# The RWKV scan: its triangular inverses taken from TensorE's five levels to a substitution on GpSimd

## The chip, the cores and the metric

The kernel runs on one core of a Trainium2 chip. The metric is the device time of one execution in microseconds (us), the median of the runs.

## The reference, cut to what matters

The program is two transformer blocks in a row. The part changed is the RWKV-7 layer: 16 heads of 64 features, 768 tokens (256 of context, then 512), scanned in both directions.

```python
def step(S, inp):
    w_t, k_t, v_t, kk_t, a_t = inp[:5]
    s_kk = jnp.einsum('nbhvk,nbhk->nbhv', S, kk_t)
    S = S * w_t[..., None, :] - s_kk[..., :, None] * (kk_t * a_t)[..., None, :] + v_t[..., :, None] * k_t[..., None, :]
    y_t = jnp.einsum('nbhvk,nbhk->nbhv', S, inp[5]) if emit else None
    return S, y_t
s_final, ys = lax.scan(step, state0, seqs)
```

The kernel does this by chunks of 64 tokens (CH). Within a chunk the dependence of each token on those before it is a unit triangular 64x64 matrix, which has to be inverted once for every head, chunk and direction: 16 x 12 x 2 of them.

## The kernel before, in words

The program is a list of stages. All engines meet between two stages (stage_done, L2995); the SP queue, which only issues DMAs, runs ahead as far as its own waits allow.

**RwkvTerms** (L2291) goes over 8 pairs of heads, m = 0 to 7 (KD). For each it makes five factors of 128x768 for either direction (decays, keys, values) and stores them to DRAM as "terms". DVE does `terms(m)` and then `factors(m+1)` (L2560); TensorE does `lora`, `norm` and `bonus` of m+1 (L2459); ACT does the exponentials and sigmoids; GpSimd does `directed` and `weighted` (L2396 to L2411); SP stores (L2364 to L2377). At the end GpSimd waits for the stores (L2428).

**RwkvScan** (L2577) makes 24 passes, three to a pair of heads. A pass n has four chunks (BATCH) in both directions d. The two heads of a pair sit on partitions 0 to 63 and 64 to 127, so each product is two 64x64 matmuls (`heads`, L2680), and `each` (L2685) does it for the four chunks: 8 matmuls. Every fp32 matmul is two instructions in the trace. In `make` (L2698) TensorE computes the products of the terms, then transposes by the identity (L2717 to L2720), and then inverts: LEVELS has five levels (2, 4, 8, 16, 32), and at each the inverse T and its transpose TT are doubled in block size by a product z (L2727), which DVE masks (L2826), and the products for T (L2737) and TT (L2738), which DVE adds (L2832, L2834). The last level needs TT alone. Then come w (L2741) and the two corrections (L2744, L2745), and DVE makes nh_h, qa and a (L2839 to L2842).

The recurrence itself is `step` (L2747): four steps per pass, each 16 matmuls, whose new state DVE scales (L2859) before the next step can run. The four steps of pass n-1 are spread between the levels of pass n, so that one fills the waits of the other; `alone` does the last four. The order is written out by hand in `make` of each engine; the instructions of one engine run in that order.

SP loads the terms of a pass in five parts of 256 KB, waiting for each (L2665 to L2669), into one of three buffers. It waits before a pass for `taken` (L2663), which DVE raises at the end of a pass (L2845), so it can be up to three passes ahead. At the start of the stage GpSimd clears the output (L2672), and DVE raises the first `taken` only behind that (L2791, L2792).

Of the kernel before, what the change touches and what calls it, by code (L numbers as in the profile page):

```python
# [47 lines left out]
CH = 64  # L48
NC = T // CH
# [152 lines left out]
def scan_constants():  # L202
# [5 lines left out]
    off = lambda s: (r // (2 * s) == c // (2 * s)) & (r // s != c // s)  # L208
    starts = np.broadcast_to(np.arange(T) % CH != 0, (P, T)).astype(np.float32)
    masks = [lo, up, r >= c, r <= c, -1.0 * (lo & off(1)), -1.0 * (up & off(1)), r == c] + [-1.0 * off(s) for s in (2, 4, 8, 16, 32)]  # L210
    return np.ascontiguousarray(np.concatenate([starts] + [two(x) for x in masks], 1))
# [2079 lines left out]
class RwkvTerms(Stage):  # L2291
# [8 lines left out]
    def __init__(self, chip):  # L2300
# [4 lines left out]
        self.starts, at = chip.view(at, T), at + T  # L2305
# [17 lines left out]
        assert at + 4 * P <= A_W  # L2323
        self.decays = chip.view(DECAYS, KD, 2, NC)
# [3 lines left out]
        self.bonus_stored = [chip.sem(f"terms_bonus_stored{u}") for u in range(2)]  # L2328
        (self.starts_in, self.scaled, self.sliced, self.lora, self.activated, self.raw_done, self.squared,
# [6 lines left out]
    STORED = 4 * 16  # L2336

# [16 lines left out]
    def sync(self, sp):  # L2354
        d = self.chip.dram
        sp.wait_ge(self.chip.stage_done, 4 * self.index)
        sp.dma_start(self.starts, d["scan_const"][:, 0:T]).then_inc(self.starts_in, 16)
# [6 lines left out]
        def store(m, u, i, more):  # L2364
# [11 lines left out]
            for b, chunks in enumerate((0, 2, 1)):  # L2376
                sp.dma_start(to[b, :, 1], flat[1][:, chunks]).then_inc(self.stored[u], 16)  # L2377

# [8 lines left out]
    def gpsimd(self, pool):  # L2387
# [40 lines left out]
        for u in range(2):  # L2428
            pool.wait_ge(self.stored[u], self.STORED * (KD // 2) + self.STORED)
            pool.wait_ge(self.bonus_stored[u], 16 * (KD // 2))  # L2430

    def tensor(self, pe):
# [30 lines left out]

        def step(m, u, i, more):
            first(m + 1, 1 - u, i)

        self.w.landed(pe, 0, 0)
        self.each(pe, first, step, nothing)
# [49 lines left out]
    def vector(self, dve):  # L2518
# [40 lines left out]

        def step(m, u, i, more):  # L2560
            terms(m, u, i)
            factors(m + 1, 1 - u, i + u)

        self.each(dve, factors, step, terms)


Y_RWKV = A_HL
LEVELS = (2, 4, 8, 16, 32)
SCAN_MASKS = ["lo", "up", "lo_diag", "up_diag", "lo1", "up1", "ident64"] + [f"level{s}" for s in LEVELS]
# [7 lines left out]
class RwkvScan(Stage):  # L2577

    def __init__(self, chip):
# [5 lines left out]
        self.t, self.tt, self.z, self.qa, self.a, self.lbt = (single(i) for i in range(6))  # L2587
        self.v = [single(i) for i in range(6, 6 + BATCHES)]
        at += (12 + 2 * BATCHES) * BATCH * CH
        double = lambda i: [chip.view(at + (2 * i + d) * BATCH * 2 * CH, BATCH, 2, CH) for d in range(2)]  # L2590
        self.p_lg, self.mb_b, self.mg_g, self.w, self.nh_h = (double(i) for i in range(5))
        at += 10 * BATCH * 2 * CH
# [464 lines left out]
```

## Time and profile before

| | |
|---|---|
| median of 3 runs | 6093.58 us (6093.32 to 6096.73) |
| the profiled execution | 6084.52 us, span 6082.9 us |
| mean granted TensorE clock | 0.935 |
| busy share of the span | PE 88%, DVE 41%, ACT 20%, POOL 7% |
| chain that ended last | PE 70%, DVE 8%, issue 7% |
| RwkvTerms | from 3237.9 us (its first DMA) to 3495.9 us |
| RwkvScan | from 3495.9 us to 4285.5 us |

PE is TensorE, DVE VectorE, ACT ScalarE, POOL GpSimd and SP the queue that issues DMAs. The span is that of the profiled execution, from its first to its last instruction.

### The profile page before, as it was taken

The numbers are of one execution on the slowest core, as the hardware profiler recorded it, in microseconds if no ns is written. First come the engines' busy times: TensorE is split into PE (matmuls) and PEld (weight loads), VectorE is DVE, ScalarE is ACT, GpSimd is POOL, SyncE is SP. The second block draws the span as 40 slices with busy tenths as digits, with TensorE's granted clock in tenths as the row PEclk, the third lists the DMA queues.
The fourth block names the chain that finished last, engine by engine and source line by source line (L and its number), as shares of the span: only waits on it lengthen the run. The fifth ranks groups of instructions, "written<-read, shape, count | busy, mean of one in ns | idle before, by whom it ended". The sixth has DMA issues, their size and how long they took to land.

```text
span 6082.9 us, 89797 instructions
## 1 busy us (share of the span) xinstructions
PE 5368.0 (88%) x36014; PEld 3112.2 (51%) x36014; DVE 2479.6 (41%) x4422; ACT 1212.2 (20%) x1969; POOL 429.9 (7%) x397
## 2 busy tenths in 40 slices
PE   7977878899999899987995389999688999999999
PEld 3556535544444345544552189999343444444443
DVE  2357644511231216733105867777514445411110
ACT  2113213300121111101004400011112333311120
POOL 0014200000000001100003400000100000000000
PEclk9989988899999999998996699999798999999999
DMA  3311330021222113420223521111110000022121
GB/s 137 101 63 69 107 104 13 35 97 55 73 76 76 48 63 131 157 90 31 82 91 141 198 60 44 47 47 30 56 45 32 19 20 17 13 69 76 61 73 69
DMA packets 92899, 428.13 MB, mean 70 GB/s; under 512 B 9952, under 2 KB 10080, under 8 KB 75104
## 3 DMA queue, kind: packets, MB, share of 16 engines
q1 hardware_dynamic: 71072, 338.34, 15.8%
q0 software_dynamic: 21568, 85.99, 4.1%
q8 instruction: 204, 3.34, 0.2%
q14 instruction: 55, 0.45, 0.0%
HBM read 364.53 MB, written 59.77 MB: 70 GB/s over the span
## 4 chain that ended last, share of the span: by engine, by line
PE 70%; DVE 8%; issue 7%; PEld 5%; DVEq 4%; DMA 3%; ACT 2%; PEldq 0%; POOL 0%; POOLq 0%; ACTq 0%; SPq 0%
PE psum L371 42%; PE psum L2682 12%; PE psum L2253 6%; PEld psum L371 4%; PE psum L1979 2%; PE psum L1978 2%; PE psum L633 1%; DMA sbuf<-w_side 1%; PE psum L2001 1%; DVEq L2530 1%; DVEq L2540 1%; PE psum L1014 1%; PE psum L1259 1%; DVE sbuf L648 1%; DVE sbuf L2956 1%
## 5 line engine op out<-in xcount | busy, mean ns | idle before, releaser
L371 PE MATMUL psum<-sbuf 128*128 128x512 f32 (+4 forms) x8640 | 3214.3, 532 | 210.3 <-DVEq L1470 61.8
L371 PEld LDWEIGHTS psum<-sbuf 128*128 128x128 f32 (+1 forms) x8640 | 1573.9, 192 | 1816.3 <-issue 1584.1
L2682 PE MATMUL psum<-sbuf 64*64 64x64 f32 (+1 forms) x21504 | 757.4, 228 | 58.7 <-SPq L2669 47.3
L2682 PEld LDWEIGHTS psum<-sbuf 64*64 64x64 f32 x21504 | 740.5, 134 | 76.2 <-issue 62.5
L2253 PE MATMUL psum<-sbuf 128*128 128x512 f32 (+1 forms) x1088 | 358.1, 490 | 30.8 <-DVE sbuf L2233 29.0
L1476 DVE SCALAR_TENSOR_TENSOR sbuf<-psum,sbuf 128x512 f32 x64 | 42.3, 682 | 660.1 <-PE psum L371 660.1
L2253 PEld LDWEIGHTS psum<-sbuf 128*128 128x128 f32 x1088 | 207.3, 191 | 181.6 <-issue 163.9
L583 DVE CUSTOM_DVE_ANT_0 sbuf<-sbuf 128x1024 f32<-128x1024 f32 x160 | 212.2, 1327 | 36.4 <-DMA sbuf<-w_side 15.8
L2772 ACT ACTIVATE sbuf<-psum 128x256 f32<-128x256 f32 x192 | 76.2, 438 | 728.7 <-PE psum L2682 727.5
L2437 PE MATMUL psum<-sbuf 64*128 64x512 f32 (+2 forms) x192 | 92.1, 739 | 145.5 <-ACT sbuf L2491 68.4
L616 ACT ACTIVATE sbuf<-sbuf 128x512 f32<-128x512 f32 (+1 forms) x114 | 53.0, 551 | 667.7 <-DVEq L2999 649.1
L664 DVE TENSOR_SCALAR sbuf<-sbuf 128x512 f32<-128x512 f32 (+1 forms) x68 | 36.2, 533 | 331.3 <-ACT sbuf L1522 189.0
L1696 POOL TENSOR_TENSOR sbuf<-sbuf 128x768 f32<-128x768 f32 (+1 forms) x32 | 45.2, 1415 | 1543.9 <-DVEq L1758 1330.7
L2095 DVE TENSOR_REDUCE sbuf<-psum 128x1 f32<-128x768 f32 x64 | 61.3, 958 | 211.4 <-PE psum L1979 211.4
L2437 PEld LDWEIGHTS psum<-sbuf 64*128 64x128 f32 (+1 forms) x192 | 40.8, 276 | 196.5 <-ACT sbuf L2491 73.1
L1746 ACT ACT_TABLE_LOAD x32 | 41.1, 1283 | 494.0 <-PEq L1731 494.0
L573 POOL DMA_DIRECT2D sbuf<-w_side x128 | 68.5, 535 | 864.6 <-DVE sbuf L583 860.8
L633 PE MATMUL psum<-sbuf 128*128 128x512 f32 (+1 forms) x228 | 92.8, 565 | 34.0 <-ACT sbuf L616 34.0
L1768 DVE SCALAR_TENSOR_TENSOR sbuf<-psum,sbuf 128x512 f32<-128x512 f32 (+1 forms) x48 | 30.3, 659 | 225.2 <-PEq L1731 220.4
L1978 PE MATMUL psum<-sbuf 128*128 128x512 f32 (+1 forms) x256 | 117.3, 541 | 3.5 <-DVE sbuf L2086 3.5
L1979 PE MATMUL psum<-sbuf 64*128 64x512 f32 (+1 forms) x256 | 119.8, 549 | 0.0
L1649 DVE TENSOR_TENSOR sbuf<-sbuf 128x512 f32 x40 | 27.7, 693 | 224.4 <-ACT sbuf L1639 224.4
(274 smaller groups left out, 4876.9 us busy)
## 6 DMA issues: line engine op xcount, KB each, us to landing
sbuf<-w_side POOLq DMA_DIRECT2D x128, 512.0 KB, 3.9
sbuf<-w_sgu_uz SPq DMA_DIRECT2D x32, 1088.0 KB, 5.0
sbuf<-terms SPq DMA_DIRECT2D x120, 256.0 KB, 2.7
sbuf<-w_up SPq DMA_DIRECT2D x22, 1024.0 KB, 4.9
sbuf<-w_merge SPq DMA_DIRECT2D x8, 2560.0 KB, 8.9
sbuf<-w_sgu_v SPq DMA_DIRECT2D x8, 2048.0 KB, 7.9
sbuf<-w_sgu_out SPq DMA_DIRECT2D x16, 1024.0 KB, 4.8
terms<-sbuf SPq DMA_DIRECT2D x8, 1920.0 KB, 11.4
```

The lines of the kernel that those rows point to most:

```text
L371: last = nc.tensor.matmul(out, w, x, start=(n == 0), stop=(n == len(pairs) - 1))
L573: pool.dma_start(self.slot[b], src).then_inc(self.landed[b], 16)
L583: last = v.tensor_tensor_reduce(junk, self.slot[b], self.rows[:, c], 1.0, 0.0, ALU.mult, ALU.add, self.sums[:, b, n:n + 1])
L633: last = self.nc.tensor.matmul(self.chip.bank(n, t), self.chip.const("ones"), squares[:, i], start=(i == 0), stop=(i == k - 1))
L648: v.reciprocal(inv, rms)
L1978: t.matmul(s[:, a:a + w], self.qn[u][:, q], self.kn[u][:, a:a + w], start=True, stop=False)
L1979: last = t.matmul(s[:, a:a + w], rot[:, q], self.kr[u][:, a:a + w], start=False, stop=True)
L2095: v.tensor_reduce(self.mx[:, n:n + 1], self.s_bank(n), AX.X, ALU.max)
L2253: last = self.nc.tensor.matmul(self.wide(b)[:, at:at + width], w[:, k], xs[:, k, at:at + width], start=(k == 0), stop=(k == KD - 1))
L2437: last = t.matmul(out[:, at:at + width], w, x[:, at:at + width], start=True, stop=True)
L2682: last = t.matmul(out[hs], lhs[hs], rhs[hs], start=start, stop=stop)
L2772: copy = lambda to, of: a.activation(to, of, ACT.Copy)
```

## The change

In RwkvTerms TensorE also makes, for each pair of heads, the two diagonal 32x32 blocks of every 64x64 triangle (12 chunks, 2 directions, 2 heads, 2 blocks: 96 matmuls with 64 rows, 32 columns and 32 elements moved). DVE masks and negates them in one operation of 128x768, and SP stores them to DRAM in four DMAs, whose contiguous runs are 32 elements (128 B).

In RwkvScan the 96 blocks of a pair are loaded so that each lies in one partition (32 x 32 elements). `substitute` inverts all of them in place by substitution: 30 steps of a product and a sum, with a drain behind either, and a transposed copy at the end. GpSimd does it for pairs 1 to 7, one pair ahead, and DVE for pair 0 at the start of the stage. SP stores both results to DRAM (384 KB each), waits, and loads them back into the layout of the matmuls with 12 DMAs of 32 partitions x 12 chunks x 128 B. `terms` in SP's new order is the load of one pass as before. TensorE keeps the level of 32 alone, as two products of 32x32 blocks, whose results ACT copies; the products of the terms are put in another order, and ACT takes over some copies. All four steps of the recurrence still stand between the parts of the next pass, and DVE raises the first `taken` before GpSimd's clearing. The masks, the smaller buffers and the new semaphores are left out of the diff:

```diff
@@ RwkvTerms.sync, at the end of store(m, u, i, more)
+            sp.wait_ge(self.blocks_out, m + 2)
+            for q in range(4):
+                sp.dma_start(blocks[q], self.blocks[u][BLK * q:BLK * q + BLK]).then_inc(self.blocks_stored[u], 16)
@@ RwkvTerms.gpsimd, at the end
+            pool.wait_ge(self.blocks_stored[u], self.BLOCKS_STORED * (KD // 2) + self.BLOCKS_STORED)
@@ RwkvTerms.tensor
+                    if (q, d) == (1, 0) and not (isinstance(m, int) and m == 0):
+                        pe.wait_ge(self.blocks_out, m)
...
+        def blocks(m, u):
+            pe.wait_ge(self.done, m + 2)
+            pe.sem_inc(self.pe_waited, 1)
+            for d, (row, col) in enumerate(((0, 2), (2, 0))):
+                o = self.out[u][d]
+                for c in range(NC):
+                    for r in range(2):
+                        for h in range(2):
+                            hs, rows, cols = slice(CH * h, CH * h + CH), CH * h + BLK * r, BLK * (NC * d + c)
+                            b = slice(BLK * r, BLK * r + BLK)
+                            last = t.matmul(self.wide(3)[rows:rows + BLK, cols:cols + BLK], o[hs, c, row, b], o[hs, c, col, b], start=True, stop=True)
+            last.then_inc(self.block_sums, 1)
+
         def step(m, u, i, more):
             first(m + 1, 1 - u, i)
+            pe.wait_ge(self.activated, 4 * m + 7)
+            pe.sem_inc(self.pe_waited, 1)
+            blocks(m, u)
@@ RwkvTerms.vector
+        def blocks(m, u, i):
+            dve.wait_ge(self.blocks_stored[u], self.BLOCKS_STORED * i + self.BLOCKS_STORED)
+            dve.wait_ge(self.block_sums, m + 1)
+            v.tensor_tensor(self.blocks[u], self.wide(3).rearrange("p (k c) -> p k c", c=BLK), across(self.strict, NBLK), ALU.mult
+                            ).then_inc(self.blocks_out, 1)
+
         def step(m, u, i, more):
             terms(m, u, i)
             factors(m + 1, 1 - u, i + u)
+            blocks(m, u, i)
@@ RwkvScan.sync
+        sp.dma_start(self.x[0], d["blocks"][0]).then_inc(self.blocks_in[0], 16)
...
+        def inverse(m):
+            u = m % 2
+            if m == 0:
+                sp.wait_ge(self.first_inverse, 1)
+            else:
+                sp.wait_ge(self.inverse_ready, m)
+            sp.dma_start(d["inverse"][m, 0], self.x[u]).then_inc(self.inverse_stored, 16)
+            sp.dma_start(d["inverse"][m, 1], self.xt[u]).then_inc(self.inverse_stored, 16)
+            sp.wait_ge(self.inverse_stored, 32 * m + 32)
+            back = [d["inverse"][m, i].rearrange("(q k) (i c) -> q i k c", q=4, c=BLK) for i in range(2)]
+            for way in range(2):
+                chunks = slice(NC * way, NC * way + NC)
+                for q in range(4):
+                    to = slice(BLK * q, BLK * q + BLK)
+                    if q % 2 == way:
+                        sp.dma_start(self.t[u][to, chunks], back[way][q, :, chunks]).then_inc(self.inverse_in[u], 16)
+                    sp.dma_start(self.tt[u][to, chunks, self.cols(q % 2)], back[1 - way][q, :, chunks]).then_inc(self.inverse_in[u], 16)
+
+        for m in range(KD):
+            terms(m, 0)
+            terms(m, 1)
+            inverse(m)
+            if m + 1 < KD:
+                sp.dma_start(self.x[(m + 1) % 2], d["blocks"][m + 1]).then_inc(self.blocks_in[(m + 1) % 2], 16)
+            terms(m, 2)
@@ RwkvScan, new method
+    def substitute(self, eng, engine, m, products):
+        x = self.x[m % 2].rearrange("p (i c) -> p i c", c=BLK)
+        xt = self.xt[m % 2].rearrange("p (i c) -> p i c", c=BLK)
+        eng.wait_ge(self.blocks_in[m % 2], 16 * (m // 2) + 16)
+        engine.memset(self.x[m % 2][:, 0:BLK * BLK:BLK + 1], 1.0)
+        for j in range(1, BLK - 1):
+            n = BLK - 1 - j
+            left = x[:, j + 1:BLK, j:j + 1].broadcast_to([4 * NBLK, n, j])
+            right = x[:, j:j + 1, 0:j].broadcast_to([4 * NBLK, n, j])
+            product = products[0:4 * NBLK, 0:n * j].rearrange("p (i c) -> p i c", c=j)
+            engine.tensor_tensor(product, left, right, ALU.mult)
+            eng.drain()
+            engine.tensor_tensor(x[:, j + 1:BLK, 0:j], x[:, j + 1:BLK, 0:j], product, ALU.add)
+            eng.drain()
+        engine.tensor_copy(xt, x.rearrange("p i c -> p c i"))
@@ RwkvScan.gpsimd
+        for m in range(1, KD):
+            self.substitute(pool, self.nc.gpsimd, m, products)
+            pool.drain().then_inc(self.inverse_ready, 1)
@@ RwkvScan.tensor, make (the removed lines are those of the listing)
+                if past:
+                    wait(self.w_out[d], n)
+                each(at(self.half(d, 1, 0)), term(0), term(3))
+                each(at(self.half(d, 1, 1)), term(3), term(1)).then_inc(self.sums[d], 1)
...
                 wait(self.made[d], n + 1)
+                each(flat(self.slots(d, 0, 2)), term(2), pq).then_inc(self.sums[d], 1)
+                each(at(self.half(d, 2, 0)), term(0), id64)
+                each(at(self.half(d, 2, 1)), term(4), id64).then_inc(self.sums[d], 1)
             if past:
                 step(*past, 0)
...
+                wait(self.evacuated[d], 2 * n + 2)
+                each(at(self.half(d, 0, 0)), term(2), id64)
+                each(at(self.half(d, 0, 1)), term(3), id64).then_inc(self.token_sums[d], 1)
+            if past:
+                step(*past, 1)
+            if pos == 0:
+                wait(self.inverse_in[m % 2], self.INVERSE_IN * (m // 2) + self.INVERSE_IN)
...
+            for s in range(BATCH):
+                for h in range(2):
+                    for d in range(2):
+                        rows = self.rows(h, d)
+                        last = t.matmul(self.narrow(d, 1)[self.rows(h, 1 - d), s], self.lbt[d][rows, s], inverse[0][d][rows, s], start=True, stop=True)
...
+            if past:
+                step(*past, 2)
             for d in range(2):
+                wait(self.z_out[d], n + 1)
+                wait(self.copied[d], n + 1)
+            for s in range(BATCH):
+                for h in range(2):
+                    for d in range(2):
+                        rows = self.rows(h, 1 - d)
+                        last = t.matmul(self.narrow(d, 2)[self.rows(h, d), s], self.z[d][rows, s], inverse[1][d][rows, s, self.cols(1 - d)], start=True, stop=True)
...
+            if past:
+                step(*past, 3)
             for d in range(2):
+                wait(self.tt_out[d], n + 1)
+                each(flat(self.slots(d, 1, 2)), at(inverse[1][d]), flat(self.p_lg[d])).then_inc(self.w_sums[d], 1)
```

On ACT each pass now copies term 0 and term 4 (128x256, twice for each direction), the two token transposes, z (128x128), the two 32-row halves of the new block of TT, and w (128x512). DVE keeps the masks of the four products of a pass, one of them (lbt) now 128x128, then the four steps, then nh_h, qa and a.

## Rows read from the trace of the kernel before

**Rows 1.** Busy time by stretch: span, then us and (instructions) of PE, PEld, DVE, ACT, POOL; PEclk, DMA share, GB/s.
```profile
3495.00:3515.50 20.50, 0.00 (x0) 0.00 (x0) 0.00 (x0) 0.00 (x0) 5.22 (x1) 0.50 0.30 85
...
3600.00:3700.00 100.00, 98.85 (x2830) 96.78 (x2832) 74.55 (x197) 9.54 (x24) 0.00 (x0) 1.00 0.16 43
```

**Rows 2.** Scan, groups by line and shape: count, busy us, mean ns, idle before.
```profile
L2682 PE MATMUL psum<-sbuf 64*64 64x64 f32 x17664 | 546.9, 218 | 10.3 <-DVEq L2843 1.2 <-issue 1.1 <-DVE sbuf L2859 0.8
L2682 PE MATMUL psum<-sbuf 64*64 64x128 f32 x3840 | 222.7, 271 | 48.4 <-SPq L2669 47.3
L2826 DVE TENSOR_TENSOR sbuf<-psum,sbuf 128x256 f32<-128x256 f32 x240 | 102.0, 425 | 14.1 <-PE psum L2682 2.8
L2772 ACT ACTIVATE sbuf<-psum 128x256 f32<-128x256 f32 x144 | 47.4, 384 | 301.4 <-PE psum L2682 300.2
L2839 DVE TENSOR_TENSOR sbuf<-sbuf,psum 128x512 f32<-128x512 f32 x48 | 33.1, 689 | 65.7 <-PE psum L2682 65.7
```

**Rows 3.** Timeline of the last steps, done alone (start us, us, engine, line).
```profile
4279.06 1.15 PE L2682 MATMUL psum<-sbuf 64*64 64x64 f32 x32 [1.19 <-DVEq L2843]
4279.86 0.48 DVE L2859 TENSOR_SCALAR sbuf<-psum,sbuf 128x64 f32<-128x64 f32 x2 [1.19 <-PE psum L2682]
...
4280.48 1.15 PE L2682 MATMUL psum<-sbuf 64*64 64x64 f32 x32 [0.27 <-DVE sbuf L2859]
```

**Rows 4.** Lines L869 and L1321, GpSimd: ns min/median/max, first and last start.
```profile
L869 POOL TENSOR_TENSOR sbuf<-sbuf x40: 1031/1042/1045, 390.3 to 480.4; 128x512 f32<-128x512 f32 x40
...
L1321 POOL TENSOR_TENSOR sbuf<-sbuf x12: 1261/1274/1732, 881.3 to 1160.2; 128x512 f32<-128x512 f32 x12
```

**Rows 5.** Timeline of GpSimd in the stage behind the scan.
```profile
4301.48 1.81 POOL L2971 TENSOR_TENSOR sbuf<-sbuf 128x768 f32 x1 [799.80 <-DVE sbuf L2960]
4303.45 1.81 POOL L2973 TENSOR_TENSOR sbuf<-sbuf 128x768 f32 x1 [0.16 <-issue]
```

**Rows 6.** Timeline of an early stage: GpSimd and DVE side by side.
```profile
520.09 1.28 POOL L970 TENSOR_TENSOR sbuf<-sbuf 128x512 f32<-128x512 f32 x1 [0.92 <-ACT sbuf L985]
...
520.15 1.13 DVE L1076 SCALAR_TENSOR_TENSOR sbuf<-psum,sbuf 128x128 f32<-128x128 f32 x4 [0.43 <-PE psum L1014]
```

**Rows 7.** Scan, groups by shape: a DVE operation with both inputs in SBUF.
```profile
L2810 DVE TENSOR_TENSOR sbuf<-sbuf 128x256 f32<-128x256 f32 x48 | 20.5, 426 | 5.3 <-issue 0.9
```

**Rows 8.** DMA issues: count, KB each, median us from issue to landing.
```profile
sbuf<-terms SPq DMA_DIRECT2D x120, 256.0 KB, 2.7
...
bonus<-sbuf SPq DMA_DIRECT2D x8, 384.0 KB, 2.3
```

**Rows 9.** DMA queue q1, 3240 to 3495 us: packets, MB, share of 16 engines.
```profile
q1 hardware_dynamic: 12212, 48.34, 49.5%
```

**Rows 10.** The same queue, 3495 to 4290 us.
```profile
q1 hardware_dynamic: 17740, 32.70, 14.5%
```

**Rows 11.** Busy time of one stretch of RwkvTerms, columns as in Rows 1.
```profile
3330.00:3360.00 30.00, 10.65 (x24) 4.67 (x24) 28.89 (x18) 18.31 (x23) 15.10 (x7) 0.61 0.52 197
```

**Rows 12.** Timeline of RwkvTerms, one turn of m.
```profile
3338.35 2.93 PE L2437 MATMUL psum<-sbuf 128*128 128x512 f32 x4 [8.94 <-ACT sbuf L2491]
...
3348.96 6.17 PE L2437 MATMUL psum<-sbuf 128*128 128x512 f32 x16 [7.68 <-POOL sbuf L2408]
...
3352.17 0.96 DVE L2541 TENSOR_TENSOR sbuf<-sbuf 128x768 f32<-128x768 f32 x1
...
3353.32 2.52 DVE L2549 TENSOR_TENSOR sbuf<-sbuf 128x768 f32<-128x768 f32 x1 [0.19 <-issue]
```

**Rows 13.** The chain that ended last, end of RwkvTerms and start of RwkvScan.
```profile
3483.71 0.33 SPq L2371
...
3486.40 9.25 DMA terms<-sbuf
...
3496.45 5.29 POOLq L2673
```

More of the change, by code:

```diff
@@ L2323, in __init__ @@
         assert at + 4 * P <= A_W
+        assert self.w.words + 2 * NBLK * BLK <= WSLOT
+        at = A_W + self.w.slot(0) * WSLOT + self.w.words
+        self.blocks = [chip.view(at + u * NBLK * BLK, NBLK, BLK) for u in range(2)]
         self.decays = chip.view(DECAYS, KD, 2, NC)
@@ L2562, in step, with last @@
             factors(m + 1, 1 - u, i + u)
-        self.each(dve, factors, step, terms)
+            blocks(m, u, i)
+        def last(m, u, i):
+            terms(m, u, i)
+            blocks(m, u, i)
+        dve.sem_inc(self.blocks_out, 1)
+        for u in range(2):
+            dve.sem_inc(self.blocks_stored[u], self.BLOCKS_STORED)
+        self.each(dve, factors, step, last)
 Y_RWKV = A_HL
-LEVELS = (2, 4, 8, 16, 32)
-SCAN_MASKS = ["lo", "up", "lo_diag", "up_diag", "lo1", "up1", "ident64"] + [f"level{s}" for s in LEVELS]
+SCAN_MASKS = ["lo_diag", "up_diag", "lo", "up", "ident64"]
 HEAD = [slice(CH * h, CH * h + CH) for h in range(2)]
@@ new lines, in sync, with terms @@
+        sp.dma_start(self.chip.view(self.masks_at, len(SCAN_MASKS) * CH), d["scan_const"][:, T + BLK:]).then_inc(self.masks_in, 16)
+        def terms(m, b):
+            sp.wait_ge(self.taken, 3 * m + b + 1)
+            src = d["terms"][3 * m + b].rearrange("p d w -> p (d w)")
+            for part in range(PARTS):
+                w = slice(part * LOAD, part * LOAD + LOAD)
+                sp.dma_start(self.terms[:, b, w], src[:, w]).then_inc(self.landed, 16)
+                sp.wait_ge(self.landed, (48 * m + 16 * b) * PARTS + 16 * part + 16)
+            sp.sem_inc(self.ready, 1)
@@ new lines, in make @@
+            inverse = [[self.of_pass(x, m, pos, d) for d in range(2)] for x in (self.t, self.tt)]
+            for d in range(2):
+                wait(self.evacuated[d], 2 * n + 1)
+            for s in range(BATCH):
[3 more added lines that the diff above has]
+                        last = t.matmul(self.narrow(d, 1)[self.rows(h, 1 - d), s], self.lbt[d][rows, s], inverse[0][d][rows, s], start=True, stop=True)
+                        if (s, h) == (BATCH - 1, 1):
+                            last.then_inc(self.z_sums[d], 1)
@@ L2766, in alone @@
                 step(*past, s)
-        self.passes(pe, make, alone, written_out=True)
+        self.passes(make, alone)
     def scalar(self, act):
@@ new lines, in make @@
+                dve.wait_ge(self.sums[d], 3 * n + 1)
+                v.tensor_tensor(self.p_lg[d][:, :, 1], self.half(d, 1, 0), self.mask(after[d]), mult)
+                v.tensor_tensor(self.mg_g[d][:, :, 0], self.half(d, 1, 1), self.mask(before[d] + "_diag"), mult)
+            for d in range(2):
+                dve.wait_ge(self.sums[d], 3 * n + 2)
+                lbt = self.slots(d, 0, 2)
+                v.tensor_scalar(self.lbt[d], lbt[:, :, 0, self.cols(1 - d)], -1.0, None, mult).then_inc(self.evacuated[d], 1)
+                v.tensor_tensor(self.mb_b[d][:, :, 0], lbt[:, :, 1], self.mask(before[d] + "_diag"), mult).then_inc(self.evacuated[d], 1)
@@ L2872, in alone @@
                 step(*past, s)
-        self.passes(dve, make, alone, written_out=True)
+        self.passes(make, alone)
 class RwkvOutput(Stage):
```

222 lines of the change are left out of this document (99 added, 123 removed).

## The prediction

> **What bounds the kernel now.** I read the busy times by stretch first, to find the stage that the change is about, then the groups by shape within it. In the scan's steady part TensorE is busy 98.85 us of 100, at the full granted clock, with DVE at 75 and ACT at 10 [rows 1]. The groups by shape say what fills it: 17,664 instructions on 64 columns, 31.0 ns of TensorE each (546.9 us over the count), and 3,840 on 128 columns, 58.0 ns each [rows 2]. A pass is a 24th of that, 736 and 160 instructions: 22.8 + 9.3 = 32.1 us, and TensorE's busy stretch, 770 us, divided by 24 gives the same. So the scan is bound by TensorE's count of instructions, and no wait in it matters but the first 20 us, where everything waits for the first terms [rows 1]. The timeline of the last steps shows what hides behind that: done alone, a step comes every 1.42 us with 1.15 us of TensorE in it [rows 3].
>
> The chain that ended last shows the seam before the scan: DVE's last terms are done at 3483.7, the last store lands at 3495.6, then GpSimd clears the output for 5.3 us, and SP's first load waits for that [rows 13]. In RwkvTerms DVE is busy 28.89 us of 30, TensorE 10.65 at a clock of 0.61 [rows 11]: DVE bounds that stage.
>
> **TensorE in the scan.** Counted from the code, in instructions (two to a matmul), the 64-column ones of a pass fall from 736 to 320 (64 for the products of two terms, 64 for transposes of terms 0 and 4, 64 for the two token transposes, 128 for the four steps), the 128-column ones from 160 to 128 (the product with two terms, w, two corrections). New are 64 on 32x32 blocks. The trace has none such; 31 ns is one end, a third of it, 10 ns, the other, and I take 20, as four of them lie on separate quarters of the array where 64x64 ones lie on two. The pass: 320 x 31.0 + 128 x 58.0 + 64 x 20 = 9.9 + 7.4 + 1.3 = 18.6 us.
>
> The waits inside a pass: z, ACT's copy, the second product, ACT's two copies for each direction, w, copy, corrections. A step of 1.15 us stands in each of the first gaps. A result reaches its reader about 0.23 us after the last matmul (DVE starts 0.80 us after a step's first, whose first half takes 0.57) [rows 3], and ACT's copies are under 0.38 us each [rows 2]. The gap behind z needs 0.23 + 2 x 0.3, covered; that behind the second product needs 0.23 + 4 x 0.25, some 0.1 over. With 0.3 for each of a few step boundaries I add 1.1 us: 19.7 a pass, 59 us for a pair of heads. DVE needs 8 masks of about 0.42, eight state scalings of 0.24, two additions and six operations behind the corrections: some 10 us of these 19.7 [rows 2, 3]. ACT needs 7. Neither bounds.
>
> Within the pass the 32x32 products change the shape of the tile four times. No row here shows such a change between products of these two shapes. If each emptied the array, at the 0.23 us above, a pass would be 20.6 us.
>
> The Trainium skill (TensorEngine Tiling (Array Packing), Key Properties) says that changing the tiling mode, not just the tile, drains TensorE. By it a pair would take 62 us on TensorE; since another loop turns out longer, the sum below would rise by about 3 us only, in the passes at both ends.
>
> **GpSimd's substitution.** 30 steps, with products and sums of j(31-j) elements each: 4,960 elements in either, 60 operations with a drain behind each. On GpSimd a plain two-input operation takes 1.274 us for 512 elements [rows 4] and 1.81 for 768 [rows 5]: 2.09 ns an element and 0.20 fixed. With one operand broadcast, as the product's is, 512 take 1.042 [rows 4]: 1.64 ns. Behind a drain the next starts 0.16 us later [rows 5]. So 4,960 x 1.64 + 4,960 x 2.09 = 18.5, 60 x 0.36 = 21.6, and 2 for the transposed copy: 42 us. The unknown is what short rows cost: 930 rows of 1 to 30 elements in all. L869 has eight rows; were its fixed 0.20 all due to them, a row costs 25 ns, and the total is 42 - 12 + 23 = 53. Below, 38 if the drain's gap overlaps. I take 42, by the rows. DVE beside it slows GpSimd only where both read two operands from SBUF: beside L1076, with one in PSUM, GpSimd's 1.28 us equals 1.274 [rows 6, 4], and DVE's operations in the new passes have one input in PSUM.
>
> **The DMAs.** The loads of a pass take 5 x 2.7 = 13.5 us of SP [rows 8]. New for each pair: two stores of 384 KB, 2.3 us [rows 8], 3 with their issues; 12 loads that are 4,608 runs of 128 B; a load of 384 KB. No row has runs of 128 B. The terms stage's queue gives 49.5% x 255 x 16 / 12,212 = 165 ns for a packet of 3.96 KB [rows 9], the scan's 14.5% x 795 x 16 / 17,740 = 104 ns for 1.84 KB [rows 10]: 29 ns a KB and 51 ns fixed, so 55 ns for 128 B, and 4,608 x 55 / 16 = 16 us. The ends are 4 us (12 issues of 0.33) and 30 (104 ns each). I take 16.
>
> **The loops.** (a) TensorE: 59. (b) GpSimd: substitution 42, then stores 3, the loads back 16, and behind them in the same queue the next pair's blocks 2.7: 64. SP can ask for those blocks only then. (c) SP: when pass 3m-2 ends it loads terms (m,1) for 13.5, stores 3, loads back 16; then the pass that waits has 10 left and one more of 19.7: 62. So 64 us a pair, with 96 before.
>
> **The start.** DVE clears TT (two of 1,536, at most 3.5 us) and substitutes pair 0: 9,920 x 1.04 ns and 60 x (0.16 + 0.10), from 0.426 us for 256 [rows 7] and 0.96 for 768 [rows 12], 27 us with the copy. SP, which no longer waits for GpSimd's clearing, has loaded two passes in the same 27 us. Then 3 + 16 + 1: the first inverse is in at about 3547; before, the first pass ended there. The end: 3547 + 7 x 64, then 10 + 2 x 19.7 for the last pair and 6.5 alone, is 4051, against 4285.5: -234.5 us.
>
> **RwkvTerms.** TensorE makes the blocks behind `bonus` of the next pair. That starts at 3348.96 and takes 2.9 us, as `norm` does for the same shapes [rows 12]. 192 instructions of 31 ns are 6 us (ends: 2, and 12 at the half clock that this stage mostly has [rows 11]). DVE, done at 3353.1 [rows 12], waits until 3358.1 and adds 1.0 us for its mask. In exchange GpSimd's two products run in that wait, and DVE's next two operations no longer take 2.5 us beside them but 0.96 [rows 12]: -3.1. Net 5.0 + 1.0 - 3.1 = 2.9 a turn, 20 us for seven (0 to 62). What was queued behind on DVE, `terms(m+1)`, is what waits. The tail: blocks 6, mask 1.2, then 3,072 runs behind the terms' stores, 10.6 us: the stage ends some 10 us later than by the chain of before [rows 13]. Together +30 (5 to 80).
>
> **Sum.** -234.5 + 30 = -204. The profiled execution's 6084.5 becomes 5880; it lies 9 us under the median shown, and against that median I forecast 5890.
>
> **Rivals.** *Small runs cost more* (chance 0.15): at 104 ns they take 30 us, the loop 78, the first inverse comes 14 later, the tail 9: 4163 in place of 4051, so about 6011. For it: nothing shows such packets; against: the line through the two rows. *The pass is latency bound* (0.1): the former cover of five levels is gone, every handover now stands once; at 24 us a pass the pair takes 72, end 4116, time 5955. For it: [rows 3]; against: the steps still stand between. *Rows cost up to 25 ns* (0.12): substitution 53, loop 75, 5967. *Slower* (0.08): short rows are dear on GpSimd, each in a pattern of its own. Break-even is where 7 more loops use up 204 us: 29 us a pair, substitution 71, 31 ns a row; at 50 ns a row it takes 88, the loop 110, and the time is 6212. TensorE then idles at `inverse_in`. Against it: L869's eight rows leave at most 25.
>
> The Trainium skill (GPSIMD Engine Reference, Performance pitfalls) gives about 102 cycles for each small read command, which does not overlap the last. If each row were such a command, the estimate from that page is 85 ns a row and a loop near 143 us. No run here shows such rows.
>
> **Numbers.** Forecast as worked out, or better, 0.55. Better: with quick loads the first inverse is in at 3535 and the loop is 59 (a): 4004, terms +5, -276, 5818. The range 5810 to 6020 takes in this and the first three rivals. About 0.2% is what a measurement of this kernel can tell from no change: faster 0.90, same 0.02, slower 0.08.
>
> **What would show it.** Right: TensorE's instructions in the scan 12,288; a pair of heads every 59 to 66 us; GpSimd's substitutions about 42 us each and busy two thirds of the scan; TensorE's busy share of it falling to some 85%; waits of DVE for TensorE of some 5 us a turn in RwkvTerms. Wrong: single operations on GpSimd well over 0.7 us with their gaps, TensorE waiting long for a DMA onto the inverse once in three passes, or gaps behind every product of a pass.

## The result, and the profile after

The changed kernel takes 5812.38 us, the median of 4 runs (5804.21 to 5822.77), against 6093.45 for the kernel before (4 runs): a ratio of 0.9539, with a 95% interval of 0.9524 to 0.9554. The profiled execution took 5804.21, with a span of 5801.8; before, the span was 6082.9. The forecast was 5890, with a range of 5810 to 6020, so the time lies 2 us inside the range's lower end, and two of the four runs lie below it: 281 us were gained where 204 had been worked out.

All of it is inside the two stages concerned. The next stage starts on TensorE at 4004.5 instead of 4285.5, 281 us earlier, and nothing behind it moved. The scan starts with its first DMA at 3500.0, 4.1 us later than before. So up to there the changed kernel is 4.1 us behind, and the scan gave 285.1. The terms stage itself takes 264.4 us instead of 258.0, from its first DMA at 3235.6 to 3500.0; it started 2.3 us earlier than before, which the change has no part in.

The busy times by stretch, in the profile after (columns as in [rows 1]):

```profile
3600.00:3700.00 100.00, 92.93 (x2609) 90.61 (x2605) 42.44 (x126) 27.01 (x81) 60.25 (x117) 0.95 0.38 100
3600.00:3900.00 300.00, 279.49 (x7871) 272.79 (x7869) 128.13 (x378) 83.26 (x249) 164.14 (x321) 0.95 0.40 103
```

TensorE was busy 98.85 us of these 100 before [rows 1]; it is now busy 92.93, at a granted clock of 0.95 instead of 1.00. DVE fell from 74.55 to 42.44. So something waits now that did not. The groups of the scan, by shape (to be set against [rows 2]; TensorE's own 64-column and 128-column forms are left together here, as the page has them, for their spans overlap):

```profile
L2805 PE MATMUL psum<-sbuf 64*64 64x64 f32 (+1 forms) x10752 | 422.9, 238 | 39.7 <-SPq L2743 28.1
...
L2865 PE MATMUL psum<-sbuf 32*32 32x32 f32 x768 | 12.5, 205 | 1.6 <-issue 0.9 <-ACT sbuf L2904 0.8
L2853 PE MATMUL psum<-sbuf 32*32 32x32 f32 x768 | 11.9, 203 | 30.9 <-DMA sbuf<-inverse 30.9
```

10,752 + 768 + 768 is 12,288 instructions, the number that was counted from the code; before there were 21,504. They take 422.9 + 12.5 + 11.9 = 447 us, 18.6 for a pass at the mean. And TensorE waits 30.9 us for a DMA onto the inverse: 8 times, once for each pair of heads. The timeline of TensorE around one such wait (start, length, instruction, count, and in brackets the wait ahead of it):

```profile
3662.07 0.65 PE L2853 MATMUL psum<-sbuf 32*32 32x32 f32 x32 [3.76 <-DMA sbuf<-inverse]
3662.66 1.97 PE L2805 MATMUL psum<-sbuf 64*64 64x64 f32 x32
3664.56 0.65 PE L2865 MATMUL psum<-sbuf 32*32 32x32 f32 x32
3665.14 17.09 PE L2805 MATMUL psum<-sbuf 64*64 64x64 f32 x416
3682.16 0.45 PE L2853 MATMUL psum<-sbuf 32*32 32x32 f32 x32
3682.54 1.15 PE L2805 MATMUL psum<-sbuf 64*64 64x64 f32 x32
3683.62 0.45 PE L2865 MATMUL psum<-sbuf 32*32 32x32 f32 x32
3684.00 15.76 PE L2805 MATMUL psum<-sbuf 64*64 64x64 f32 x416
3699.70 0.45 PE L2853 MATMUL psum<-sbuf 32*32 32x32 f32 x32
```

From 3682.16 to 3699.70 lies a pass that nothing disturbs: 17.54 us, with no gap in it. The pass that follows the wait takes 20.09 (3662.07 to 3682.16). The busy times by stretch say why; the column that counts is the third from the end, the granted clock:

```profile
3662.10:3668.00 5.90, 5.90 (x140) 5.66 (x142) 1.63 (x6) 1.52 (x6) 2.60 (x9) 0.50 0.49 144
3668.00:3674.00 6.00, 6.00 (x129) 5.87 (x127) 3.04 (x7) 1.19 (x2) 4.70 (x10) 1.00 0.33 90
```

After 3.76 us without work TensorE is granted 0.50, the lower of its two levels (1.2 GHz), for about 6 us, and then 1.00 again. So this wait costs 3.76 us itself and 2.55 by the clock. Three passes of 17.54 are 52.6; a pair of heads takes 58.2 (the first product with an inverse starts at 3543.96 for pair 0 and at 3951.30 for pair 7, a seventh of the difference).

What TensorE waits for is at the end of SP's work for the pair. The timeline of SP, the same columns (issues without a wait of their own between them are drawn together):

```profile
3541.95 44.11 SPq L2741 DMA_DIRECT2D sbuf<-terms  x15
3588.72 0.34 SPq L2751 DMA_DIRECT2D inverse<-sbuf  x1
3589.10 0.43 SPq L2752 DMA_DIRECT2D inverse<-sbuf  x1
3593.16 0.32 SPq L2760 DMA_DIRECT2D sbuf<-inverse  x1
...
3599.95 0.47 SPq L2761 DMA_DIRECT2D sbuf<-inverse  x1
3600.46 1.18 SPq L2768 DMA_DIRECT2D sbuf<-blocks  x1
3601.68 6.82 SPq L2741 DMA_DIRECT2D sbuf<-terms  x3
```

and what SP waited for in the scan (total, times, longest):

```profile
SPq L2741 <- DMA sbuf<-terms: 251.3, 96, 4.2
SPq L2743 <- DMA sbuf<-terms: 61.3, 24, 3.2
...
SPq L2760 <- DMA inverse<-sbuf: 29.5, 8, 5.1
SPq L2741 <- DVEq L2972: 3.0, 4, 1.6
```

SP never rests. It issues a part of the terms, waits until it has landed, issues the next: 15 parts in the 46.8 us from 3541.95 to 3588.72, 3.1 each. The stores are waited for until 3593.16 (4.4), the loads back and the blocks' load are issued until 3601.6 (8.5), and the next part follows at once. That is 59.7 us for this pair, where the mean pair takes 58.2. For `taken`, which says that a buffer is free, it waits 3.0 us in the whole scan. GpSimd in the meantime:

```profile
3545.61 0.15 POOL L2777 MEMSET sbuf<- 96x32 f32 x1 [39.82 <-DMA sbuf<-blocks]
3545.69 0.24 POOL L2783 TENSOR_TENSOR sbuf<-sbuf 96x30 f32<-96x30 f32 x1
3546.07 0.26 POOL L2785 TENSOR_TENSOR sbuf<-sbuf 96x30 f32<-96x30 f32 x1
```

The substitution runs from 3545.6 to 3586.2, 40.6 us (40.7 in most pairs), and GpSimd then waits 18.6 for its next blocks. SP came to the store at 3588.7, 2.5 us after the inverse was ready, and in the whole scan it never waits for GpSimd there. So in this profile it is not GpSimd's loop that sets the pair but SP's own list of waited transfers, which the prediction had added up only in part. That is the theory which the experiments below test; its rivals are GpSimd's loop, as forecast, and the short runs of the loads back.

In the terms stage the profile after shows:

```profile
3348.22 2.93 PE L2452 MATMUL psum<-sbuf 128*128 128x512 f32 x4 [7.69 <-POOL sbuf L2422]
3351.07 2.79 PE L2493 MATMUL psum<-sbuf 64*32 64x32 f32 x192
...
3351.42 0.96 DVE L2576 TENSOR_TENSOR sbuf<-sbuf 128x768 f32<-128x768 f32 x1
3354.00 0.96 DVE L2598 TENSOR_TENSOR sbuf<-psum,sbuf 128x768 f32<-128x768 f32 x1 [1.62 <-PE psum L2493]
```

The 192 instructions for the blocks take 2.79 us, 14.5 ns each at a granted clock of 0.50, and DVE waits 1.62 for them in this turn. In the turn where the clock was 0.90 they take 1.99, 10.4 ns each.

### The profile page after: what moved, and what is told of

The parts are those of the page before. It is cut to its first block, busy times and chain, and to the rows that moved or that the text cites. A ratio compares the mean times of both kernels' runs of the same rounds, so it can differ in the third digit from the quotient of the medians.

```text
span 5801.8 us, 74255 instructions
## 1 busy us (share of the span) xinstructions
PE 5067.3 (87%) x28334; PEld 2816.2 (49%) x28334; DVE 2134.7 (37%) x3582; ACT 1263.7 (22%) x2161; POOL 650.0 (11%) x831
## 4 chain that ended last, share of the span: by engine, by line
PE 65%; issue 9%; DVE 7%; DMA 7%; PEld 5%; ACT 2%; DVEq 2%; POOL 1%; SPq 1%; POOLq 1%; PEldq 0%; ACTq 0%
PE psum L373 44%; PE psum L2255 6%; PEld psum L373 5%; DMA sbuf<-terms 3%; PE psum L2805 3%; PE psum L1981 2%; PE psum L1980 2%; PE psum L635 1%; DMA sbuf<-w_side 1%; PE psum L2003 1%; PE psum L1016 1%; DVE sbuf L650 1%; PE psum L1261 1%; DVE sbuf L3083 1%; SPq L2761 1%
## 5 line engine op out<-in xcount | busy, mean ns | idle before, releaser
L2805 PE MATMUL psum<-sbuf 64*64 64x64 f32 (+1 forms) x10752 | 422.9, 238 | 39.7 <-SPq L2743 28.1
L2805 PEld LDWEIGHTS psum<-sbuf 64*64 64x64 f32 x10752 | 411.9, 138 | 46.3 <-issue 33.0
L1478 DVE SCALAR_TENSOR_TENSOR sbuf<-psum,sbuf 128x512 f32 x64 | 42.3, 682 | 660.9 <-PE psum L373 660.9
L2904 ACT ACTIVATE sbuf<-psum 128x256 f32<-128x256 f32 (+3 forms) x384 | 128.5, 368 | 395.1 <-PE psum L2805 315.3
L2785 POOL TENSOR_TENSOR sbuf<-sbuf 96x30 f32<-96x30 f32 (+14 forms) x210 | 109.1, 520 | 30.4 <-issue 0.9
```

The source lines that it names most:

```text
L2785: engine.tensor_tensor(x[:, j + 1:BLK, 0:j], x[:, j + 1:BLK, 0:j], product, ALU.add)
L2805: last = t.matmul(out[hs], lhs[hs], rhs[hs], start=start, stop=stop)
L2904: copy = lambda to, of: a.activation(to, of, ACT.Copy)
```

## The experiments

The stages ahead of the scan differ in length between executions (the first product with an inverse starts between 3540 and 3560 in the profiles), and the times of one kernel spread over 13 to 35 us. So beside the time of each kernel the table has, from its profile, the scan's own length from that product to the next stage's first matmul.

| kernel | time, us | ratio to before, 95% | scan, us | PE waits for the inverse, us | POOL waits for blocks, us |
|---|---|---|---|---|---|
| changed kernel | 5812.38 | 0.9539 (0.9524 to 0.9554) | 460.6 | 30.9 | 144.7 |
| one wait a pass (e2) | 5800.23 | 0.9534 (0.9513 to 0.9554) | 450.2 | 19.0 | 133.1 |
| half the substitution (e3) | 5821.09 | 0.9551 (0.9534 to 0.9569) | 459.4 | 25.8 | 256.2 |
| both of these (e4) | 5800.29 | 0.9507 (0.9486 to 0.9527) | 439.4 | 7.3 | 231.9 |
| blocks a pair sooner (e5) | 5812.39 | 0.9527 (0.9510 to 0.9544) | 465.5 | 35.7 | 84.9 |
| one wait, blocks sooner (e6) | 5794.02 | 0.9504 (0.9491 to 0.9518) | 438.3 | 8.9 | 56.7 |
| long runs (e7, one run) | 5797.72 | | 457.1 | 27.9 | 137.1 |

Of the waits for the inverse the first, ahead of pair 0 (8.9 us in the changed kernel), lies ahead of the scan's own length. Each ratio is to the runs of the kernel before that were made beside it; the ratios, and not the medians, are to be compared between rows.

**The terms stage alone (e1).** RwkvTerms of the changed kernel with the scan of the kernel before, which does not read the blocks.

```diff
 class RwkvTerms: as in the changed kernel
 class RwkvScan: as in the kernel before (LEVELS and the masks too)
```

> The kernel of before with the new RwkvTerms alone: the blocks are made and stored, the scan inverts as before and never reads them. My step (TensorE's 192 instructions delay DVE by 5 us a turn, net 2.9, tail 10) gives +30 us on before, about 6123. The rival, read from the trace of the changed kernel (192 instructions take 2.8 us, DVE waits 1.6 and gets its time back because GpSimd's two products no longer run beside it; the stage ends 4 us later), gives +4 us, about 6097.

Measured: 6102.23 us, the median of 12 runs, against 6092.02 (17 runs); ratio 1.0014, 1.0002 to 1.0026, which is 8.5 us, from 1 to 16. The +30 of the prediction is refuted. The turns explain it, read from the profile of the changed kernel: SP's issues of `bonus` stand 29.4 or 29.6 us apart before (3306.13, 3335.70, 3365.09) and 29.5 to 29.7 after (3334.95, 3364.50, 3394.17), but for one turn of 30.9 (from 3304.05); the last turn is 30.5 in both. In e1's own profile that one turn is 32.0 and the others are as before. DVE's groups in the terms stage show the trade, before and after:

```profile
L2550 DVE TENSOR_TENSOR sbuf<-sbuf 128x768 f32<-128x768 f32 x16 | 28.1, 1754 | 0.0
L2549 DVE TENSOR_TENSOR sbuf<-sbuf 128x768 f32<-128x768 f32 x16 | 26.5, 1655 | 2.8 <-issue 2.4 <-ACT sbuf L2507 0.4
```

```profile
L2584 DVE TENSOR_TENSOR sbuf<-sbuf 128x768 f32<-128x768 f32 x16 | 21.9, 1366 | 0.4 <-ACT sbuf L2542 0.4
L2585 DVE TENSOR_TENSOR sbuf<-sbuf 128x768 f32<-128x768 f32 x16 | 20.0, 1251 | 0.0
...
L2598 DVE TENSOR_TENSOR sbuf<-psum,sbuf 128x768 f32<-128x768 f32 x8 | 7.7, 958 | 16.7 <-PE psum L2493 16.7
```

These are the same two operations, whose span beside GpSimd's products is long. The waits (16.7) and the new mask (7.7) add 24.4 us in eight turns; the two groups lose 54.6 - 41.9 = 12.7, and DVE's idle time ahead of them another 2.4. Of the 9.3 us that remain, 7 are the wait and the mask behind the last pair's terms, in the tail, and some 2 lie in the seven turns, most of them in the long one. In that turn TensorE stops for 1.56 us in the midst of the blocks (2.66 in e1), and in the tail for 2.71, and waits for nothing that the profile shows; see below.

**Twice the blocks' matmuls (e8).** If DVE's time beside GpSimd pays part of each wait back, doubling the wait's cause must cost less than its own length.

```diff
@@ tensor, blocks(m, u), on top of e1
-            for d, (row, col) in enumerate(((0, 2), (2, 0))):
+            for d, (row, col) in 2 * list(enumerate(((0, 2), (2, 0)))):
```

> The kernel of before with the new RwkvTerms alone, whose block matmuls are issued twice (384 instructions a turn). Theory of the trade (what DVE waits for TensorE it gets back from GpSimd, whose two products run meanwhile, and by now only 1 us of that is left): 2.8 us more of TensorE, 1.8 us more a turn. Without a trade: 2.8 us more a turn. The tail grows by 2.8 in both.

Measured, in one run: 6122.27. Four turns are undisturbed. In them the 384 instructions take 4.17 to 4.68 us, 4.46 at the mean, where 192 take 2.00 to 2.79 in e1, 2.45 at the mean: 2.0 us more, and not the 2.8 of the expectation. The turns take 29.9 to 30.4 us, 30.2 at the mean, against 29.6 in e1. DVE waits 3.3 us for the blocks in such a turn instead of 1.3, so some 1.4 of these 2.0 us come back. The two operations that took 54.6 us before take 42.3 in e1 and 33.4 here; all 32 of them at the 0.95 us of the shortest would be 30.4.

Two turns were longer, 34.6 and 37.1, and TensorE's gaps in them wait for nothing in the profile:

```profile
3338.28 2.12 PE L2494 MATMUL psum<-sbuf 64*32 64x32 f32 x181
3343.89 1.93 PE L2494 MATMUL psum<-sbuf 64*32 64x32 f32 x128 [3.50 <-issue]
3347.89 1.27 PE L2494 MATMUL psum<-sbuf 64*32 64x32 f32 x75 [2.07 <-issue]
...
3374.93 4.17 PE L2494 MATMUL psum<-sbuf 64*32 64x32 f32 x384
```

The profiles say where such gaps stand. The turns for m = 0 and 1 run the loop's code for the first time and those for 2 to 5 repeat it; the last two pairs are written out behind the loop. In e8 there are gaps in m = 0, 1, 6 and 7 and none in 2 to 5; in the changed kernel and in e1 they are in m = 1, 6 and 7. The pieces between them are equal: 117 instructions and 75 in the second turn of both, 154 and 38 for m = 6, 90 and 102 for m = 7, and 128 between two gaps in e8. So they stand at fixed places of the program, and only where it is run for the first time. Why TensorE stops there was not tried.

**One wait for the five parts (e2).** SP issues a pass's five parts and waits once.

```diff
@@ sync, terms(m, b)
                 sp.dma_start(self.terms[:, b, w], src[:, w]).then_inc(self.landed, 16)
-                sp.wait_ge(self.landed, (48 * m + 16 * b) * PARTS + 16 * part + 16)
+            sp.wait_ge(self.landed, (48 * m + 16 * b) * PARTS + 16 * PARTS)
             sp.sem_inc(self.ready, 1)
```

> The changed kernel, but SP issues the five parts of a pass's terms together and waits once. Theory SP (a pair lasts as long as SP's own chain: 15 loads waited for one by one, 44 us, stores 4.4, 12 loads back and the blocks 8, then the first load again): that chain falls to some 30 us and GpSimd's loop (40.7 + 15) is next, so a pair takes 56 in place of 58.4 and the time is 5790 (-20 us). Theory GpSimd (its loop of substitution and blocks already sets 58.4) and theory TensorE (waits within the passes): no change, 5812.

Measured: 5800.23, 12 us less, though the intervals of the ratios overlap; the scan is 10.4 us shorter in the profiles, where theory SP had expected 20 us less and theory GpSimd nothing. SP's waits have changed their kind:

```profile
SPq L2743 <- DMA sbuf<-terms: 109.4, 24, 5.7
SPq L2741 <- DVEq L2972: 107.5, 14, 11.7
SPq L2751 <- POOLq L2795: 51.2, 7, 8.5
```

SP now waits for free buffers and, for the first time, 51.2 us for GpSimd's inverse. The pair takes (3937.63 - 3540.72) / 7 = 56.7, and GpSimd's loop is what is left: it ends its copy, SP stores at once, and the next blocks are in 16 us later.

```profile
3694.87 1.97 POOL L2787 COPY sbuf<-sbuf 96x1024 f32<-96x1024 f32 x1
3712.66 0.15 POOL L2777 MEMSET sbuf<- 96x32 f32 x1 [15.83 <-DMA sbuf<-blocks]
```

40.7 + 15.8 is 56.5, the pair within 0.2. So the forecast loop is real, but it lies 1.5 us behind SP's.

**Half the substitution (e3), and both (e4).** GpSimd does 15 of the 30 steps; the inverses are incomplete, all else is done.

```diff
-    def substitute(self, eng, engine, m, products):
+    def substitute(self, eng, engine, m, products, last=BLK - 1):
...
-        for j in range(1, BLK - 1):
+        for j in range(1, last):
...
-            self.substitute(pool, self.nc.gpsimd, m, products)
+            self.substitute(pool, self.nc.gpsimd, m, products, BLK // 2)
```

> The changed kernel, but GpSimd does the substitution for the first 15 of its 30 steps only (half the elements), so the inverses of pairs 1 to 7 are incomplete. Theory SP: no change, 5812, and GpSimd waits 38 us for each load of blocks in place of 18. Theory GpSimd: 20 us less a pair as far as TensorE's 52.6 (three passes of 17.54), so -40 us, 5772.

> Both edits together: one wait for a pass's terms, and half the substitution on GpSimd (incomplete inverses). Theory SP, with GpSimd next: both loops are short, a pair takes TensorE's 52.6 us, TensorE never waits for the inverse after the first pair and keeps the full clock: 5769. Theory GpSimd alone: the same as with half the substitution, 5772. Theory TensorE: 5812.

Measured: e3 takes 5821.09, and its interval overlaps that of the changed kernel; the scan 459.4 against 460.6. GpSimd is busy 87.26 us of 300 instead of 164.14, and its waits for blocks rise from 144.7 to 256.2 us: all that it saved it waits. Were its loop the bound, as forecast, the pair would have come down to the next loop's length. With one wait too (e4) the scan falls to 439.4, below either alone, and TensorE waits for an inverse once, at the start. That one edit alone does nothing, the other half, and only both together take all the waits away is what two loops of nearly one length look like. This rests on the waits and the scan's length in the profiles: e4's time, 5800.29, is that of e2, with overlapping intervals, and 31 us above the 5769 that was expected for it. What is left is below.

**Blocks loaded a pair sooner (e5), and with one wait (e6).** The other way to shorten GpSimd's loop: the blocks of pair m+2 are asked for as soon as pair m's inverse has been stored, ahead of the loads back.

```diff
@@ sync, inverse(m)
                 sp.wait_ge(self.first_inverse, 1)
+                sp.dma_start(self.x[1], d["blocks"][1]).then_inc(self.blocks_in[1], 16)
...
             sp.wait_ge(self.inverse_stored, 32 * m + 32)
+            if m + 2 < KD:
+                sp.dma_start(self.x[u], d["blocks"][m + 2]).then_inc(self.blocks_in[u], 16)
...
             inverse(m)
-            if m + 1 < KD:
-                sp.dma_start(self.x[(m + 1) % 2], d["blocks"][m + 1]).then_inc(self.blocks_in[(m + 1) % 2], 16)
```

> The changed kernel, but SP loads the blocks of a pair one pair sooner, as soon as their buffer has been stored, so that GpSimd never waits for them: its loop shrinks from 57 us to its own 41. SP still waits for each part of the terms. Theory SP (its own chain of 58 us sets the pair): no change, 5812. Theory GpSimd: 5772 to 5790.

> The blocks one pair sooner, and one wait for a pass's terms. Both loops are now shorter (SP some 32 us, GpSimd 41) than TensorE's three passes (52.6 by the undisturbed pass, 54 as seen where half the substitution was left out). So no wait of TensorE for the inverse after the first pair, a pair every 54 us, and the full clock: 5790, as with both edits before, but with whole inverses. Rival: the wait was not the loops but the DMAs' contention, then it stays at the 5800 of one wait alone.

Measured: e5 alone changes nothing, 5812.39, and SP still waits 246.8 us for its parts (its profile is of its longest execution, 5825.0, with a scan 5 us longer; the median is the changed kernel's). e6 gives 5794.02 where 5790 was expected, with a ratio of 0.9504, 0.9491 to 0.9518, which does not meet the changed kernel's: by the ratios some 21 us better than the change, with nothing left out, and the best kernel here. The rival, that the transfers' contention and not the loops made the wait, had expected the 5800 of e2; e6's scan is 11.9 us shorter than e2's, with no wait for an inverse behind the first. In its profile TensorE is all but full again:

```profile
3600.00:3900.00 300.00, 293.28 (x8541) 286.40 (x8539) 138.43 (x410) 88.84 (x266) 177.05 (x340) 1.00 0.39 107
...
3549.76:3608.58 58.82, 54.83 (x1473) 53.23 (x1473) 23.20 (x68) 16.06 (x48) 46.47 (x86) 0.93 0.42 119
...
3720.74:3773.36 52.62, 52.62 (x1535) 51.60 (x1536) 24.97 (x74) 16.06 (x48) 31.63 (x62) 1.00 0.44 113
```

The last line is a stretch of three passes, 52.62 us or 3 x 17.54, TensorE busy throughout. From first product to first product the first pair takes 58.8, since the clock is low behind the only wait for an inverse (8.9 us), and the others 52.8 to 55.7, with gaps in TensorE of 0.2 to 1.3 us in most passes, for which the profile names no releaser:

```profile
3629.94 0.21 PE L2866 MATMUL psum<-sbuf 32*32 32x32 f32 x1 [0.70 <-issue]
...
3647.86 0.26 PE L2866 MATMUL psum<-sbuf 32*32 32x32 f32 x7 [0.21 <-issue]
```

These two stand in passes 4 and 5, counted from 0, ahead of the last 1 and the last 7 instructions of the second product; in passes 6 and 7 it is the last 13 and 19. The changed kernel has gaps at the same instructions (pass 4 at 3624.19, pass 5 at 3642.35), and so has e4 (passes 4, 6 and 7). So these too stand at fixed places of the program; TensorE's code in the scan is written out, so each place is run once. Added up over the passes they are 3.2 us in the changed kernel and 3.2 to 4.8 in e3, e5 and e7, but 7.3 in e2, 11.2 in e6 and 13.1 in e4, where SP asks for five parts at once. In the longer scan of before, whose code on TensorE is written out too, they are 1.2. Their cause was not tried.

They have a price. From the changed kernel to e6 22.0 us of waits in the scan go away, and TensorE's busy time, for the same 12,064 instructions, falls by 8.4 us with the clock (the first line is the changed kernel's, the second e6's). Still the scan is only 22.3 us shorter, since the gaps take some 8 back:

```profile
3543.96:4004.52 460.56, 430.55 (x12064) 419.82 (x12065) 198.71 (x584) 125.82 (x376) 225.04 (x434) 0.96 0.36 93
```

```profile
3549.76:3988.04 438.28, 422.12 (x12064) 411.17 (x12065) 198.70 (x584) 125.94 (x376) 216.63 (x414) 0.99 0.35 96
```

**Long runs (e7).** The 12 loads back take the same bytes as rows of 1536 B instead of 128 B; the inverse's values land in the wrong places.

```diff
-                        sp.dma_start(self.t[u][to, chunks], back[way][q, :, chunks]).then_inc(self.inverse_in[u], 16)
+                        sp.dma_start(flat_t[to, run * way:run * way + run], back[way][BLK * (q // 2):BLK * (q // 2) + BLK, 0:run]).then_inc(self.inverse_in[u], 16)
```

> The changed kernel, but each of the 12 loads of the inverses moves the same bytes as 32 runs of 1536 B in place of 384 of 128 B (so wrong elements arrive). My step (55 ns for each short run, 16 us for all) gives 4608 - 384 = 4224 runs less and some 11 us less from the first load's issue to TensorE's product. The rival read from the trace (the loads are bound by SP's issue, 0.47 us each, and the runs overlap): some 2 us less, through 0.33 us an issue, and a pair shorter by as much.

Measured, in one run: 5797.72; the scan 457.1, 3.5 us shorter. SP's issue of a load takes 0.42 instead of 0.47, and from the first issue to TensorE's start 7.0 to 9.7 us pass, 8.2 at the mean of the eight pairs (3648.65 to 3656.70 for pair 2), where they were 8.3 to 9.8, 9.2 at the mean (3652.23 to 3662.07 for pair 2). So the short runs cost about 1 us a pair, and not the 11 that the step of the prediction gives. The one time of 5797.72 tells nothing by itself: executions of the changed kernel went from 5804 to 5823, those of e5 from 5790 to 5825. In the changed kernel's chain of waits the loads are a row of issues, and only the last transfer shows:

```profile
3531.45 3.98 DMA inverse<-sbuf
3535.45 0.32 SPq L2760
...
3540.41 0.47 SPq L2760
3540.93 2.99 DMA sbuf<-inverse
3543.96 0.67 PE psum L2853 x26
```

## Why the prediction was right in its sign and short by 77 us

The sum of the prediction can be redone from the profile after, term by term. It gave the scan -234.5; the profile has -285.1.

- **The instruction count** was right: 12,288, and TensorE's busy share of 3600 to 3900 is 93%, over the 85 that was named, since the pair is shorter.
- **The pass** was 2.2 us too long: 19.7 forecast, 17.54 measured. The 64 instructions on 32x32 blocks take 0.38 us for 32, 12 ns each (from one shape's start to the next one's, 3682.16 to 3682.54), near the lower end of 10 and not 20: 0.5 us. The 1.1 us for handovers did not come: in an undisturbed pass the step of 1.15 us covers ACT's copies behind either product. The rest, 0.5, is in the 64- and 128-column ones.
- **The change of tile shape** was given 0.23 us in one bound. The rows show 32 instructions of 64x64 starting 0.38 us behind the start of 32 on 32x32, and the step between the two as long as before, 1.15 us [rows 3]. The Trainium skill (TensorEngine Tiling (Array Packing), Key Properties) has a drain at every change of the tiling mode; this trace does not agree, as far as gaps of some 0.05 us can be told from it.
- **GpSimd's substitution** was right: 40.7 us for 42. The short rows cost nothing of their own: the first step's operations have 30 rows of one element in each of 96 partitions and take 0.24 us. At 25 ns a row they would take 0.75. So both rivals that hung on short rows fall, with the slower case. The Trainium skill (GPSIMD Engine Reference, Performance pitfalls for Q7 kernels) has each small read command at about 102 cycles, from which the prediction estimated 85 ns a row; by that these operations would take 2.6 us, and no row here shows such a cost.
- **The loops are the step that failed.** "So 64 us a pair" is 58.2. Two terms of (b) were off: the loads back, 16 us from the line through two rows of other packets, take 7.0 in e2 until their last issue has been made, and e7 shows that the short runs are about 1 us of it; and with stores (4.8) and the blocks' load (4.0) the rest of the loop is 15.8 in e2, not 21.7. That alone makes (b) some 56.7. What then binds is a loop that the prediction did not list: under (c) it counted one pass's loads of the three and TensorE's passes for the rest. But every part is waited for, so SP's whole list is serial: 15 parts in 46.8 us, 4.4 for the stores and 8.5 of issues in the pair shown, and it has no slack. It was within reach: 15 x 2.7 [rows 8] + 3 + 16 = 60 by the prediction's own prices, just under its 64. Seven pairs at 5.8 less are 41 us.
- **The start.** DVE's substitution took 25.3 (27 forecast), the stores 4.4 (3), the loads back 8.5 (17 with the last step). Against the scan's own start the first product comes 44.0 us in, where the forecast had 51.1: 7 us. The end, from the last pair's first product, took 53.2 and not 55.9: 3 us.
- **RwkvTerms**: +4.1 at its end in the profiles (the stage alone +6.4) and +8.5 in e1's runs, where 30 was forecast. The blocks' matmuls were priced at 31 ns and took 10 to 14.5 (2.0 to 2.8 us a turn, not 6), within the bounds of 2 and 12. The trade of DVE's wait against its slow operations beside GpSimd was forecast and is there. The turns, 20 us in the forecast, cost 2: from the first issue of `bonus` to the last 209.2 us instead of 207.0. The tail, 10 in the forecast, costs 4: the last store lands at 3499.8, 16.1 us after the last issue of `bonus`, instead of 3495.6, 11.9 after it. 2.7 us of the tail are TensorE's gap in the last blocks.

41 + 7 + 3 in the scan and 26 up to its start are the 77 us; 2.3 of these 26 are the earlier start of the terms stage. The time is nearest to the forecast's "or better" case, 5818 with the first inverse at 3535 and the pair at 59, but that is luck: the first inverse came 44.0 us into the scan and not 39, and the pair of 58.2 is held by SP's list and not by TensorE's loop (a), which is 52.6. The time lies in the range, and the loop that sets it was not in the sum. One of the signs of "wrong" is there in a small form: once in three passes TensorE waits for a DMA onto the inverse, 1.6 to 5.4 us; the forecast's own loops of 59 and 64 imply 5. Of the rivals, small runs at 104 ns are refuted by e7, the latency-bound pass by the pass of 17.54.

**A rise that was not priced.** A wait of TensorE costs more than its length. Of the 58.2 - 52.6 = 5.6 us that a pair takes beyond its three passes, 3.2 are waiting, some 1.7 come in the pass behind the wait, mostly through the lower clock, and 0.7 are small gaps in the other two passes. e6 shows the clock at 1.00 over 300 us where the change has 0.95. What that gave back, the gaps took again.

**What stays open.** The cause of TensorE's gaps of 0.2 to 1.7 us in e4 and e6, and of those in the long turns of e8, beyond their place in the program; a version whose passes repeat in a loop, or e6 with fewer transfers at once, would test it. And the first 44 us of the scan, in which TensorE has little to do until the first inverse is in. That none of the versions shortens by more than 2.4 us (from the scan's first DMA to the first product it is 41.6 us in e2, 44.8 in e5).

## What to carry to other kernels

When the engine that bound a stage is relieved, add up every queue's own list for one round, waits included, and not only the loops that the change makes: a queue of transfers that are each waited for costs transfers times landing time, and it shows no idle time that anything else would be blamed for. Where two loops are within a few per cent of each other, test them with both edits apart and together, for either alone shows nothing or half. Price a new wait of TensorE with the clock behind it, and when such waits are taken away look at what else grows before the gain is counted.

## What was not expected of the hardware

- TensorE granted 0.50 for about 6 us after 3.76 us of idleness in the midst of full work, at a cost of 2.55 us on top of the wait. Other waits did so in part: in the 5 to 6 us behind waits of 2.44 and 2.59 us (changed kernel) and of 2.27, 2.84 and 3.42 (e2) the granted clock was 0.66 to 0.72, behind waits of 1.61, 1.69 and 1.95 it was 1.00. The length alone does not order them: behind 5.36 us it was 0.70, behind 3.35 it was 0.50 (changed kernel).
- 12 ns for an instruction on a 32x32 block, and for one with 64 rows and 32 columns 10.4 at a granted clock of 0.90 and 14.5 at 0.50, with no visible gap at either change of shape.
- Gaps of TensorE at the same instructions of the program in different kernels: in the terms stage only where a loop's code runs for the first time or is written out, none in the turns that repeat it.
- A DMA of 384 runs of 128 B costs SP 0.47 us to issue against 0.42 for 32 rows of 1536 B, and lands in 2.2 us against 1.9 at the median.
- GpSimd's operations on rows of a few elements take as long as their element count says, 0.24 us for 30 and 0.61 for 240 in a product with a broadcast operand.
